# Moving the second half of an input projection behind the state product of a hybrid mixer

## The chip, the cores and the metric

The kernel runs on one core of one Trainium2 chip. The metric is the device time of one execution in microseconds (us); lower is better. The core has a matmul engine (TensorE, PE in the rows; its weight loads are PEld), VectorE (DVE), ScalarE (ACT), GpSimd (POOL), and SyncE (SP), which issues the weight transfers. PE writes its results into eight PSUM banks, numbered 0 to 7.

## The reference, cut to what matters

The program is a two-layer network followed by a second network whose first layer holds a hybrid mixer. Only that mixer is touched. For 256 tokens (two tiles of 128) it computes:

```python
def hybrid_mixer(h, w_in, conv_w, ...):
    z, xbc, dt_raw, q, k, v, f_raw = jnp.split(h @ w_in, offs, axis=-1)
    xbc = jax.nn.silu(causal_conv(xbc, conv_w, conv_b))
    xs, bm, cm = jnp.split(xbc, ...)
    y = ssd_chunked(xh, dt, a, bm, cm)        # state-space branch
    y = (y + d_skip * xh) * silu(z)           # then normed: y_ssm
    o = forgetting_attention(q, k, v, log_f)  # 8 heads of 128, causal
    return jnp.concatenate([y_ssm, o], axis=-1) @ w_out

def forgetting_attention(q, k, v, log_f):     # per block of 128 queries
    logits = q @ k * d ** -0.5 + cum[query] - cum[key]
    return softmax(where(causal, logits, -inf)) @ v
```

## The kernel before

**Products.** Every product is in f32 out of two rounded halves: a weight block is cut into an upper part (ScalarE, the `cut` of `scalar_program`) and a rest (VectorE, the `cut` of `vector_program`), and `three` issues three matmuls: upper by upper, upper by rest, rest by upper. Weights come in halves of 128x1024. One half of a 512-column block is 12 matmuls (two row groups `f`, two token tiles, three products). `W.span["hyb.z7"]` are the four halves of the last input block, and `W.span["hyb.out0"]` are the first halves of the output product. Four slots hold cut weights, so a half is cut at most three ahead of its use (`cut_ahead`).

**The mixer.** The input product has the blocks z0 to z7. Blocks z2 and z3 are the queries, z4 and z5 the keys, z6 and z7 the values; z7 holds the values of heads 4 to 7. Small pieces of work stand between the halves of z4 to z7, listed in the tables called `work` on each of the three engines, by number 4*(block-4)+half. After z7 PE runs `within(0)` (first tile of the state-space branch), the state product (event `hyb.S0`, banks 0 and 1), `within(1)`, the product with the state (`hyb.yo`), and then the attention, by hand, unit by unit. A unit is four heads of one query tile: units 0 and 1 are heads 0 to 3, units 2 and 3 heads 4 to 7; odd units have 256 keys, even ones 128. `front(i)` is the scores on PE, scale, bias and maximum on VectorE (events `fox{i}.sc`, `fox{i}.max`), the exponentials on ScalarE (`fox{i}.p`); `middle(i)` transposes the weights on PE and copies them out on ScalarE; `back(i)` is the product with the values. `queries(hg)` and `keys(hg)` transpose queries and keys (copies by `turned` on ScalarE); `y_parts` transposes the normed state-space rows, and `y_hi` and `y_lo` cut them; `out_halves` is the output product; `added` on VectorE builds the additive bias of the scores.

**What sets the order.** Each engine runs its own list in order. `free(banks)` makes PE wait until the last result in a bank was read; `held` notes who reads it. For scores that is VectorE's `fox{i}.sc`. The state product waits, besides its inputs, for banks 0 and 1, where the scores of unit 0 lie.

Of the kernel before, what the change touches and what calls it, by code (L numbers as in the profile page):

```python
# [17 lines left out]
P = 128  # L18
# [206 lines left out]
def build(nc, io, learned):  # L225
# [203 lines left out]
        return [dict(name=f"{l}.xat{t}", scale=P ** -0.5, add=None, dv=P, nk=TT, t=t, place=IN_ORDER,  # L429
                     value=lambda h, kt: z[:, kt, XV + h * P:XV + (h + 1) * P], dst=heads(ostage[:, t, :], 4)) for t in range(TT)]  # L430

    QT, KTs = [ostage[:, :, :].rearrange("p t (a n) -> p (t a) n", a=2), tT[:, 8:12, :]], [acc[:, 0:4, :], nT[:, 4:8, :]]
    xt = [z[:, t, H_X:H_X + D] for t in range(TT)]
    R = [[tT[:, 12 + 4 * t:16 + 4 * t, :] for t in range(TT)], [xt[t].rearrange("p (h k) -> p h k", h=4) for t in range(TT)]]
    heads_out = [[ostage[:, t, :] for t in range(TT)], [z[:, t, H_Q:H_Q + 512] for t in range(TT)]]

    def fox_units():
        return [dict(name=f"fox{2 * hg + t}", scale=P ** -0.5, add=R[hg][t][:, :, 0:(t + 1) * P], dv=P, nk=t + 1, t=t, hg=hg, place=IN_ORDER,
# [58 lines left out]
    def tensor_program():  # L497
# [171 lines left out]

            return lambda c, t: buf[:, t, at + c * P:at + (c + 1) * P]  # L670

        def attention(units, scores, ready, values=(), first=None, beside={}, by_act=False, between=None, amid={}, rear_banks=(6, 7), behind={}, within={}, by_hand=False):

            n_ = len(units)

            def front(i):
                b = 2 * (i % 2)
                free(b, b + 1)
                for p in ready(i):
                    PE.wait_ge(*p)  # L680
                o = ps[:, b:b + 2, :].rearrange("p a (h k) -> p (a h) k", h=2)
                u_ = units[i]
                scores(u_, o).then_inc(*psum_full.up(f"{u_['name']}.s"))
                held(act_out.at(f"{u_['name']}.p") if u_["add"] is None else dve_out.at(f"{u_['name']}.sc"), b, b + 1)

            def middle(i):
                s, n = i % 2, units[i]["name"]
                PE.wait_ge(*act_out.at(f"{n}.p"))
                free(4, 5)
                nk = units[i]["nk"]  # L690
                for h in range(4):
                    for kt in range(nk):
                        m = PE.transpose(ps[:, 4 + h // 2, (h % 2 * nk + kt) * P:(h % 2 * nk + kt + 1) * P], S[:, s, h, kt * P:(kt + 1) * P], ident)  # L693
                m.then_inc(*psum_full.up(f"{n}.t"))
                held(act_out.at(f"{n}.PT") if by_act else dve_out.at(f"{n}.PT"), 4)
                held(act_out.at(f"{n}.PT"), 5)

            def back(i):
                s, b, u_ = i % 2, rear_banks[i % len(rear_banks)], units[i]
                n, dv, nk = u_["name"], u_["dv"], u_["nk"]  # L700
                if not by_act:
                    PE.wait_ge(*dve_out.at(f"{n}.PT"))
                PE.wait_ge(*act_out.at(f"{n}.PT"))
                free(b)
                for p in values:
                    PE.wait_ge(*p)
                for h in range(4):
                    for kt in range(nk):
                        m = PE.matmul(ps[:, b, h * dv:(h + 1) * dv], PTs[:, s, nk * u_["place"][h] + kt, :], u_["value"](h, kt), start=(kt == 0), stop=(kt == nk - 1))  # L709
                    if h == 1 and i in within:  # L710
                        within[i]()
                m.then_inc(*psum_full.up(f"{n}.o"))
                held(dve_out.at(f"{n}.out"), b)

            if by_hand:
                return front, middle, back

            front(0)
            if between:
                between()  # L720
            front(1)
            if first:
                first()

            def rear(i):
                back(i)
                if i in beside:
                    beside[i]()
            for i in range(n_):
                middle(i)  # L730
                if i in amid:
                    amid[i]()
                if i + 2 < n_:
                    front(i + 2)
                if i + 2 in behind:
                    behind[i + 2]()
                if i:
                    rear(i - 1)
            rear(n_ - 1)
# [369 lines left out]
        def hybrid(then):  # L1109
# [54 lines left out]
            def to_rows(t):  # L1164
                PE.wait_ge(*act_out.at("hyb.silu"))
                for q, (first, n_) in enumerate(row_sets):
                    b = row_banks[q]
                    free(b)
                    for i in range(n_):
                        m = PE.transpose(ps[:, b, i * P:(i + 1) * P], tT[:, first + i, TOK[t]], ident)  # L1170
                    m.then_inc(*psum_full.up(f"hyb.rows{t}{q}"))
                    held(act_out.at(f"hyb.rows{t}{q}"), b)
# [12 lines left out]
            def keys(hg):  # L1185
                turn(f"hyb.K{hg}", cols_of(z, H_K + 512 * hg), 4, [act_out.at(f"hyb.z{4 + hg}")], lambda c: act_out.at(f"hyb.K{hg}.{c}"))

            work = {0: sums, 2: lambda: to_rows(0), 5: lambda: to_rows(1), 7: products, 12: lambda: queries(0), 13: lambda: keys(0)}
            def scores(u_, o):
                for h in range(4):  # L1190
                    keys_ = slice(0, u_["nk"] * P)
                    m = PE.matmul(o[:, h, keys_], QT[u_["hg"]][:, h, TOK[u_["t"]]], KTs[u_["hg"]][:, h, keys_], start=True, stop=True)
                return m
            front, middle, back = attention(fox_units(), scores, lambda i: [act_out.at(f"hyb.K{i // 2}.2"), act_out.at(f"hyb.Q{i // 2}.2")], by_act=True,
                                            rear_banks=(0, 7, 6, 7), by_hand=True)
            work[15] = lambda: front(0)
            for b in range(4, 8):
                banks = (2 * (b % 2), 2 * (b % 2) + 1)
                gemm(f"hyb.z{b}", lhs, banks, beside=lambda n_: work.get(4 * (b - 4) + n_, lambda: None)())
                held(act_out.at(f"hyb.z{b}"), *banks)  # L1200

            def within(t):
                PE.wait_ge(*dve_out.at(f"hyb.W{t}"))
# [15 lines left out]
            held(act_out.at("hyb.S0"), 0, 1)  # L1219
            within(1)  # L1220
            PE.wait_ge(*act_out.at("hyb.S0"))
            free(2, 3)
            for g in range(2):
                m = PE.matmul(ps[:, 2 + g, :], CT[:, g, P:2 * P], S0[:, g * 512:(g + 1) * 512], start=True, stop=True)
            m.then_inc(*psum_full.up("hyb.yo"))
            held(dve_out.at("hyb.yo"), 2, 3)


            def out_halves(first, last):
# [13 lines left out]
            def y_parts(*groups_):  # L1243
                for c in groups_:
                    part_group("hyb.yT", cols_of(z), 8, c, [act_out.at("hyb.ynorm"), dve_out.at("hyb.ynorm")], (6, 7, 1, 3))
            queries(1)
            keys(1)
            front(1)
            middle(0)
            front(2)  # L1250
            front(3)
            middle(1)
            y_parts(0, 2)
            back(0)
            y_parts(4)
            middle(2)
# [121 lines left out]
    def vector_program():  # L1378
# [152 lines left out]
            V.tensor_tensor(block_of(x, hf), block_of(x, hf), o, ALU.add).then_inc(*dve_out.up(event))  # L1531


        def attention(units, out, first=None, beside={}, by_act=False, between=None, second=None, amid={}, rear_banks=(6, 7), by_hand=False):

            def front(i):
                s, b, u_ = i % 2, 2 * (i % 2), units[i]
                keys = slice(0, u_["nk"] * P)
                n, o = u_["name"], ps[:, b:b + 2, :].rearrange("p a (h k) -> p (a h) k", h=2)[:, :, keys]
                Su, nm = S[:, s, :, keys], rs[:, s, 0, :]  # L1540
# [450 lines left out]
        def hybrid():  # L1991
# [64 lines left out]
            def added(hg, tokens=range(TT)):  # L2056
                own()
                V.wait_ge(*keys_loaded.at(hg))
                for t in tokens:
# [6 lines left out]

            work = {0: sums, 4: lambda: state_inputs(0), 5: lambda: decays(0), 7: lambda: decays(1), 8: lambda: state_inputs(1), 9: lambda: skipped(0), 10: to_end,
                    11: lambda: weigh(0), 12: lambda: skipped(1), 13: lambda: weigh(1), 14: lambda: added(0)}
            for b in range(4, 8):
                cuts(f"hyb.z{b}", lambda n: work.get(4 * (b - 4) + n, lambda: None)())  # L2070

            def within(t):
                V.wait_ge(*psum_full.at(f"hyb.y{t}"))
                own()
                for g in range(2):
                    V.tensor_tensor(xt[t][:, g * 512:(g + 1) * 512], xt[t][:, g * 512:(g + 1) * 512], ps[:, y_banks[t][g], :], ALU.add).then_inc(*dve_out.up(f"hyb.y{t}{g}"))
            front, middle, back = attention(fox_units(), plain_out, by_act=True, rear_banks=(0, 7, 6, 7), by_hand=True)
            own()
            front(0)
            within(0)  # L2080
# [1 line left out]
            own()  # L2082
            V.tensor_tensor(z[:, 0, 0:D], z[:, 0, 0:D], xt[0], ALU.mult).then_inc(*dve_out.up("hyb.zy0"))
            V.wait_ge(*psum_full.at("hyb.yo"))
            V.tensor_tensor(heads(yo), ps[:, 2:4, :].rearrange("p a (h d) -> p (a h) d", h=8), bc(eacs, 64), ALU.mult).then_inc(*dve_out.up("hyb.yo"))

            def second_tokens():
                own()
# [153 lines left out]
    def scalar_program():  # L2242
# [460 lines left out]
        def hybrid():  # L2703
# [63 lines left out]

            def last_decays():
                decays(1, 11, 16)
                turned("Q", 0, QT)  # L2770

            def products():
# [3 lines left out]
            def turned(kind, hg, dst):  # L2776
                for c in (0, 2):
                    pair_to(f"hyb.{kind}{hg}", c, dst[hg][:, c:c + 2, :], 6 + c // 2)

            work = {0: sums, 2: lambda: to_rows(0), 3: spread_rows, 5: lambda: to_rows(1), 6: lambda: decays(0, 0, 4), 7: first_half, 8: lambda: decays(0, 8, 12), 9: lambda: decays(0, 12, 16),  # L2780
                    10: lambda: decays(1, 0, 6), 11: lambda: decays(1, 6, 11), 12: last_decays, 13: lambda: turned("K", 0, KTs)}
            for b in range(4, 8):
                cuts(f"hyb.z{b}", lambda n: work.get(4 * (b - 4) + n, lambda: None)())
                A.wait_ge(*product(f"hyb.z{b}"))
                scaled(f"hyb.z{b}", block_of(z, 3 + b), ps[:, 2 * (b % 2):2 * (b % 2) + 2, :])
            A.wait_ge(*psum_full.at("hyb.S0"))
            A.copy(S0, ps[:, 0:2, :].rearrange("p a b -> p (a b)")).then_inc(*act_out.up("hyb.S0"))
            def y_squares(t):
# [27 lines left out]
            front(1)  # L2816
            y_parts()
            middle(1)
            front(2)
            y_hi(0, 2)  # L2820
            y_hi(4)
# [383 lines left out]
```

## Time and profile before

| | us |
|---|---|
| runs, median of 3 | 2071.18 |
| runs, lowest and highest | 2071.17 and 2074.01 |
| profiled execution, its own time | 2073.56 |
| span of the profiled execution | 2072.1 |
| granted clock of the profiled execution, mean | 0.997 |

The span runs from the first instruction to the last one; the 1.5 us between it and the execution's own time lie around it. All times in rows count from the start of the span. The part that is changed lies between 1334 and 1392 us.

### The profile page before, as it was taken

How to read it: one execution, taken by the hardware profiler on the slowest of the kernel's cores; microseconds unless marked ns; L12 is line 12 of the kernel's file. 1: busy time of each engine (PE TensorE's matmuls, PEld its weight loads, DVE VectorE, ACT ScalarE, POOL GpSimd, SP SyncE). 2: the span in 40 equal slices, each digit the busy share in tenths (PEclk: the TensorE clock that was granted, in tenths of full speed). 3: DMA queues.
4: the chain of work that ended last, by engine and by line, in shares of the span. 5: the costliest groups of instructions: out<-in, count | busy, mean ns of one | idle time of the engine just before them, and what ended most of it. 6: DMA issues, size and time to landing. Idle time of an engine off the chain costs nothing.

```text
span 2072.1 us, 27212 instructions
## 1 busy us (share of the span) xinstructions
PE 2044.6 (99%) x10690; PEld 1723.7 (83%) x10690; DVE 1431.9 (69%) x2056; ACT 1180.3 (57%) x1906; POOL 65.8 (3%) x101
## 2 busy tenths in 40 slices
PE   9999999999999999999999999999999999999998
PEld 7877888888887788888888888878888888887887
DVE  6987756764698875676577557776765766587763
ACT  5547566553546656555465457755554655486552
POOL 0001100000000200000000000000000000010000
PEclk9999999999999999999999999999999999999999
DMA  7572344555555244455455554515555555545553
GB/s 251 198 247 100 144 164 149 191 196 183 186 202 213 92 163 158 154 198 183 183 203 193 185 212 183 214 68 195 185 184 200 186 192 186 203 151 192 186 199 123
DMA packets 54902, 372.56 MB, mean 180 GB/s; under 512 B 7471, under 2 KB 7767, under 8 KB 11128
## 3 DMA queue, kind: packets, MB, share of 16 engines
q1 hardware_dynamic: 49392, 356.54, 47.5%
q10 hardware_dynamic: 4872, 12.70, 1.9%
q0 software_dynamic: 512, 1.57, 0.3%
q8 instruction: 86, 1.41, 0.3%
q14 instruction: 40, 0.33, 0.0%
HBM read 369.46 MB, written 1.34 MB: 179 GB/s over the span
## 4 chain that ended last, share of the span: by engine, by line
PE 92%; ACT 3%; DVE 3%; DMA 1%; issue 1%; POOL 0%; SPq 0%; DVEq 0%; ACTq 0%; POOLq 0%
PE ps L567 21%; PE ps L519 17%; PE ps L523 17%; PE ps L520 17%; PE ps L573 11%; PE ps L709 1%; DMA ring<-in_w 1%; PE ps L602 1%; PE ps L642 1%; PE ps L658 1%; PE ps L693 1%; DVE ring_lo L1386 1%; ACT S L2392 1%; ACT upper_w L2254 0%; PE ps L1207 0%
## 5 line engine op out<-in xcount | busy, mean ns | idle before, releaser
L1386 DVE TENSOR_TENSOR ring_lo<-ring,upper_w 128x1024 fp32r<-128x1024 f32 x435 | 525.4, 1222 | 202.7 <-ACT upper_w L2254 201.6
L2254 ACT CAST upper_w<-ring 128x1024 fp32r<-128x1024 f32 x435 | 449.3, 1050 | 277.6 <-DMA ring<-in_w 163.3
L520 PE MATMUL ps<-ring_lo,nT_pair 128*128 128x512 f32 (+1 forms) x984 | 382.2, 388 | 0.0
L519 PE MATMUL ps<-upper_w,nT_pair 128*128 128x512 f32 (+1 forms) x848 | 337.4, 398 | 2.2 <-DVE ring_lo L1386 1.5
L523 PE MATMUL ps<-upper_w,nT_pair 128*128 128x512 f32 (+1 forms) x680 | 265.4, 390 | 0.0
L573 PEld LDWEIGHTS ps<-nT_pair,ring_lo 128*128 128x128 f32 x1920 | 246.2, 191 | 9.4
L573 PE MATMUL ps<-nT_pair,ring_lo 128*128 128x256 f32 x1920 | 249.0, 283 | 0.0
L520 PE MATMUL ps<-ring_lo,z_hi 128*128 128x512 f32 x624 | 242.9, 389 | 0.0
L567 PE MATMUL ps<-nT_pair,upper_w 128*128 128x512 f32 x960 | 230.0, 391 | 0.0
L520 PEld LDWEIGHTS ps<-ring_lo,nT_pair 128*128 128x128 f32 x984 | 185.6, 189 | 35.3
L567 PEld LDWEIGHTS ps<-nT_pair,upper_w 128*128 128x128 f32 x960 | 176.5, 188 | 34.2
L523 PE MATMUL ps<-upper_w,tT_lo 128*128 128x512 f32 (+1 forms) x528 | 204.8, 388 | 0.0
L519 PEld LDWEIGHTS ps<-upper_w,nT_pair 128*128 128x128 f32 x848 | 159.9, 189 | 38.6 <-issue 3.5
L1386 DVE TENSOR_TENSOR ring_lo<-ring,PT_w 128x1024 fp32r<-128x1024 f32 x112 | 134.9, 1220 | 55.2 <-ACT PT_w L2254 55.2
L1386 DVE TENSOR_TENSOR ring_lo<-ring,S_w 128x1024 fp32r<-128x1024 f32 x112 | 134.7, 1219 | 46.5 <-ACT S_w L2254 46.5
L2254 ACT CAST PT_w<-ring 128x1024 fp32r<-128x1024 f32 x112 | 115.5, 1050 | 70.0 <-DMA ring<-in_w 70.0
L2456 ACT COPY z<-ps 128x512 f32<-128x512 f32 x60 | 35.2, 587 | 207.6 <-PE ps L573 207.6
L523 PEld LDWEIGHTS ps<-upper_w,nT_pair 128*128 128x128 f32 x680 | 127.9, 188 | 27.3 <-DVE nT_pair L1448 0.7
L1618 DVE TENSOR_TENSOR acc<-ps,z 128x512 f32<-128x512 f32 x60 | 41.5, 692 | 156.0 <-ACT z L2456 156.0
L2254 ACT CAST S_w<-ring 128x1024 fp32r<-128x1024 f32 x112 | 115.5, 1050 | 55.8 <-DMA ring<-in_w 55.6
L519 PE MATMUL ps<-upper_w,z_hi 128*128 128x512 f32 x360 | 142.1, 395 | 0.0
L520 PEld LDWEIGHTS ps<-ring_lo,z_hi 128*128 128x128 f32 x624 | 117.3, 188 | 23.4
(389 smaller groups left out, 2876.7 us busy)
## 6 DMA issues: line engine op xcount, KB each, us to landing
ring<-in_w SPq DMA_DIRECT2D x338, 1024.0 KB, 4.8
big<-in_gains ACTq DMA_DIRECT2D x7, 512.0 KB, 4.2
z<-in_mem ACTq DMA_DIRECT2D x2, 1024.0 KB, 7.5
big<-skew POOLq DMA_DIRECT2D x8, 192.0 KB, 6.7
x<-in_x SPq DMA_DIRECT2D x2, 512.0 KB, 7.4
ring<-in_w SPq DMA_DIRECT2D x2, 512.0 KB, 7.0
PTs<-skew ACTq DMA_DIRECT2D x1, 1024.0 KB, 4.6
big<-skew ACTq DMA_DIRECT2D x1, 1024.0 KB, 8.8
```

Source lines behind the costliest of these rows:

```text
L519: PE.matmul(out, hi, w_hi, start=start, stop=False)
L520: PE.matmul(out, hi, w_lo, start=False, stop=False)
L523: return PE.matmul(out, lo, w_hi, start=False, stop=stop)
L567: PE.matmul(ps[:, base + i, :], upper(W.halves[h][2])[:, cols], nT_pair[:, :, 2 * c + k, :], start=(c == 0 and k == 0), stop=False)
L573: m = PE.matmul(ps[:, base + i, 0:T], w_lo[:, cols], nT_hi[:, 2 * c + k, :], start=False, stop=(2 * c + k == KT - 1))
L602: m = PE.transpose(ps[:, b, i * P:(i + 1) * P], src[:, t, (4 * g + i) * P:(4 * g + i + 1) * P], ident)
L642: m = PE.transpose(ps[:, b, (i * TT + t) * P:(i * TT + t + 1) * P], src(c + i, t), ident)
L658: m = PE.transpose(ps[:, b, (i * TT + t) * P:(i * TT + t + 1) * P], src(c + i, t), ident)
L1386: V.tensor_tensor(ring_lo[:, q % RING, cols], ring[:, q % RING, cols], upper(n).bitcast(F32), ALU.subtract).then_inc(*lo_cut.up(h))
L1618: V.tensor_tensor(pair(b), ps[:, base:base + 2, 0:T], ffn_half[:, 0:2, :], ALU.add).then_inc(*dve_out.up())
L2254: A.copy(upper(n), ring[:, q % RING, part * HALF:(part + 1) * HALF]).then_inc(*hi_cut.up(h))
L2456: A.copy(ffn_half[:, 0:2, :], ps[:, base:base + 2, T:2 * T]).then_inc(*act_out.up(f"{f}.hg{b}"))
```

## The change

The last two halves of z7 leave the loop over the input blocks. PE now runs: z4 to z6; `queries(0)`; the first half of z7; `keys(0)`; the second half; `front(0)`; `within(0)`, the state product, `within(1)`, `hyb.yo`; the third half of z7; `queries(1)`, `keys(1)`, `front(1)`, `middle(0)`, `front(2)`; the fourth half; `middle(1)`, `y_parts(0, 2)`, and only then `front(3)`. Since z7 sums up in banks 2 and 3 over this whole time, `hyb.yo` moves to banks 0 and 1, and the units' scores lie in the banks that start at 0, 0, 0 and 2. ScalarE reads z7 out (`scaled`) between `middle(1)` and `front(2)`. The cuts: during z7 only two are made (the fourth half of z7, the first of the output product); the second and third half of the output product are cut where so far only the fourth was, after `y_hi(6)` and `y_lo(6)`. The transposed keys of heads 4 to 7 move from `nT`, which the late halves still read, to the second tile of `xn`.

```diff
--- before.py
+++ after.py
@@ -429,10 +429,12 @@
-    QT, KTs = [ostage[:, :, :].rearrange("p t (a n) -> p (t a) n", a=2), tT[:, 8:12, :]], [acc[:, 0:4, :], nT[:, 4:8, :]]
+    QT, KTs = [ostage[:, :, :].rearrange("p t (a n) -> p (t a) n", a=2), tT[:, 8:12, :]], [acc[:, 0:4, :], xn[:, 1, :].rearrange("p (c n) -> p c n", n=T)]
     xt = [z[:, t, H_X:H_X + D] for t in range(TT)]
...
     heads_out = [[ostage[:, t, :] for t in range(TT)], [z[:, t, H_Q:H_Q + 512] for t in range(TT)]]
+
+    FOX_BANKS = (0, 0, 0, 2)
@@ -669,12 +671,12 @@
-        def attention(units, scores, ready, values=(), first=None, beside={}, by_act=False, between=None, amid={}, rear_banks=(6, 7), behind={}, within={}, by_hand=False):
+        def attention(units, scores, ready, values=(), first=None, beside={}, by_act=False, between=None, amid={}, rear_banks=(6, 7), behind={}, within={}, by_hand=False, front_banks=None):
...
             def front(i):
-                b = 2 * (i % 2)
+                b = 2 * (i % 2) if front_banks is None else front_banks[i]
                 free(b, b + 1)
@@ -1185,19 +1187,35 @@
-            work = {0: sums, 2: lambda: to_rows(0), 5: lambda: to_rows(1), 7: products, 12: lambda: queries(0), 13: lambda: keys(0)}
+            work = {0: sums, 2: lambda: to_rows(0), 5: lambda: to_rows(1), 7: products, 11: lambda: queries(0)}
             def scores(u_, o):
...
             front, middle, back = attention(fox_units(), scores, lambda i: [act_out.at(f"hyb.K{i // 2}.2"), act_out.at(f"hyb.Q{i // 2}.2")], by_act=True,
-                                            rear_banks=(0, 7, 6, 7), by_hand=True)
-            work[15] = lambda: front(0)
-            for b in range(4, 8):
+                                            rear_banks=(0, 7, 6, 7), by_hand=True, front_banks=FOX_BANKS)
+            for b in range(4, 7):
                 banks = (2 * (b % 2), 2 * (b % 2) + 1)
...
                 held(act_out.at(f"hyb.z{b}"), *banks)
+
+            def last_values(c):
+                h = W.span["hyb.z7"][c]
+                w_hi, w_lo = weights(h)
+                if c == 0:
+                    free(2, 3)
+                for k in range(2):
+                    f, cols = 2 * c + k, slice(k * BLK, (k + 1) * BLK)
+                    for t in range(TT):
+                        m = three(ps[:, 2 + t, :], lhs[0](f, TOK[t]), lhs[1](f, TOK[t]), w_hi[:, cols], w_lo[:, cols], f == 0, f == KT - 1)
+                m.then_inc(*half_used.up(h))
+                if c == 3:
+                    held(act_out.at("hyb.z7"), 2, 3)
+            last_values(0)
+            keys(0)
+            last_values(1)
+            front(0)
@@ -1219,11 +1237,11 @@
             PE.wait_ge(*act_out.at("hyb.S0"))
-            free(2, 3)
+            free(0, 1)
             for g in range(2):
-                m = PE.matmul(ps[:, 2 + g, :], CT[:, g, P:2 * P], S0[:, g * 512:(g + 1) * 512], start=True, stop=True)
+                m = PE.matmul(ps[:, g, :], CT[:, g, P:2 * P], S0[:, g * 512:(g + 1) * 512], start=True, stop=True)
             m.then_inc(*psum_full.up("hyb.yo"))
-            held(dve_out.at("hyb.yo"), 2, 3)
+            held(dve_out.at("hyb.yo"), 0, 1)
@@ -1243,14 +1261,16 @@
                     part_group("hyb.yT", cols_of(z), 8, c, [act_out.at("hyb.ynorm"), dve_out.at("hyb.ynorm")], (6, 7, 1, 3))
+            last_values(2)
             queries(1)
...
             front(2)
-            front(3)
+            last_values(3)
             middle(1)
             y_parts(0, 2)
+            front(3)
             back(0)
@@ -1531,10 +1551,10 @@
-        def attention(units, out, first=None, beside={}, by_act=False, between=None, second=None, amid={}, rear_banks=(6, 7), by_hand=False):
+        def attention(units, out, first=None, beside={}, by_act=False, between=None, second=None, amid={}, rear_banks=(6, 7), by_hand=False, front_banks=None):
...
             def front(i):
-                s, b, u_ = i % 2, 2 * (i % 2), units[i]
+                s, b, u_ = i % 2, 2 * (i % 2) if front_banks is None else front_banks[i], units[i]
                 keys = slice(0, u_["nk"] * P)
@@ -2066,15 +2086,19 @@
                     11: lambda: weigh(0), 12: lambda: skipped(1), 13: lambda: weigh(1), 14: lambda: added(0)}
-            for b in range(4, 8):
+            for b in range(4, 7):
                 cuts(f"hyb.z{b}", lambda n: work.get(4 * (b - 4) + n, lambda: None)())
+            for n, h in enumerate(W.span["hyb.z7"]):
+                if n < 2:
+                    cut_ahead(h)
+                work.get(12 + n, lambda: None)()
...
                     V.tensor_tensor(xt[t][:, g * 512:(g + 1) * 512], xt[t][:, g * 512:(g + 1) * 512], ps[:, y_banks[t][g], :], ALU.add).then_inc(*dve_out.up(f"hyb.y{t}{g}"))
-            front, middle, back = attention(fox_units(), plain_out, by_act=True, rear_banks=(0, 7, 6, 7), by_hand=True)
+            front, middle, back = attention(fox_units(), plain_out, by_act=True, rear_banks=(0, 7, 6, 7), by_hand=True, front_banks=FOX_BANKS)
             own()
@@ -2082,7 +2106,7 @@
             V.wait_ge(*psum_full.at("hyb.yo"))
-            V.tensor_tensor(heads(yo), ps[:, 2:4, :].rearrange("p a (h d) -> p (a h) d", h=8), bc(eacs, 64), ALU.mult).then_inc(*dve_out.up("hyb.yo"))
+            V.tensor_tensor(heads(yo), ps[:, 0:2, :].rearrange("p a (h d) -> p (a h) d", h=8), bc(eacs, 64), ALU.mult).then_inc(*dve_out.up("hyb.yo"))
@@ -2767,6 +2791,10 @@
                 decays(1, 11, 16)
+                turned("K", 0, KTs)
+
+            def more_decays():
+                decays(1, 6, 11)
                 turned("Q", 0, QT)
@@ -2778,11 +2806,14 @@
             work = {0: sums, 2: lambda: to_rows(0), 3: spread_rows, 5: lambda: to_rows(1), 6: lambda: decays(0, 0, 4), 7: first_half, 8: lambda: decays(0, 8, 12), 9: lambda: decays(0, 12, 16),
-                    10: lambda: decays(1, 0, 6), 11: lambda: decays(1, 6, 11), 12: last_decays, 13: lambda: turned("K", 0, KTs)}
-            for b in range(4, 8):
+                    10: lambda: decays(1, 0, 6), 11: more_decays}
+            for b in range(4, 7):
                 cuts(f"hyb.z{b}", lambda n: work.get(4 * (b - 4) + n, lambda: None)())
...
                 scaled(f"hyb.z{b}", block_of(z, 3 + b), ps[:, 2 * (b % 2):2 * (b % 2) + 2, :])
+            cut_ahead(W.span["hyb.z7"][0])
+            last_decays()
+            cut_ahead(W.span["hyb.z7"][1])
             A.wait_ge(*psum_full.at("hyb.S0"))
@@ -2816,6 +2847,8 @@
             middle(1)
+            A.wait_ge(*product("hyb.z7"))
+            scaled("hyb.z7", block_of(z, 10), ps[:, 2:4, :])
             front(2)
```

## Rows read from the trace of the kernel before

**Rows 1.** First part of the page: busy us, share, instructions.
```profile
PE 2044.6 (99%) x10690; PEld 1723.7 (83%) x10690; DVE 1431.9 (69%) x2056; ACT 1180.3 (57%) x1906; POOL 65.8 (3%) x101
```
**Rows 2.** PE's timeline: start us, us, engine, line, operation, operands, count [idle before].
```profile
1337.10 1.03 PE L642 MATMUL ps<-const,z 128*128 128x128 f32 x8
...
1340.71 1.04 PE L642 MATMUL ps<-const,z 128*128 128x128 f32 x8
...
1347.08 1.06 PE L1192 MATMUL ps<-acc,ostage 128*128 128x128 f32 x8
1347.97 3.68 PE L1207 MATMUL ps<-xn,PTs 128*128 128x64 f32 x32
1351.49 1.94 PE L1217 MATMUL ps<-big,z 128*128 128x512 f32 x4
...
1358.55 1.04 PE L642 MATMUL ps<-const,z 128*128 128x128 f32 x8
...
1360.82 1.89 PE L1192 MATMUL ps<-acc,ostage 128*128 128x256 f32 x8
```
**Rows 3.** Windows: stretch, length, busy PE, PEld, DVE, ACT, POOL, granted clock, DMA.
```profile
140.00:142.00 2.00, 2.00 (x10) 1.51 (x8) 2.00 (x4) 1.08 (x2) 0.00 (x0) 0.50 1.02 418
...
1364.00:1368.00 4.00, 2.26 (x11) 1.53 (x9) 3.93 (x9) 3.52 (x12) 1.01 (x1) 1.00 0.01 2
...
1372.00:1375.00 3.00, 1.01 (x7) 0.70 (x7) 2.06 (x5) 2.77 (x9) 0.00 (x0) 1.00 0.01 3
1375.60:1379.00 3.40, 3.40 (x17) 3.30 (x16) 2.91 (x6) 1.98 (x8) 0.00 (x0) 0.50 0.02 5
```
**Rows 4.** The chain of waits, 1363 to 1378: start us, us, engine and line.
```profile
1363.88 1.15 DVE S L1543
...
1366.31 2.08 ACT S L2392 x8
1368.38 1.23 ACT z L2806 x2
1369.61 0.98 ACT PTs L2399
1370.58 1.54 ACT S L2392 x8
...
1372.94 1.67 DVE tT_lo L1427 x4
1374.75 2.97 PE ps L709 x16
```
**Rows 5.** ScalarE's timeline before the state product.
```profile
1335.84 1.25 ACT L2370 ACTIVATE z<-ps,st 128x512 f32<-128x512 f32 x2
1336.98 1.04 ACT L2254 CAST upper_w<-ring 128x1024 fp32r<-128x1024 f32 x1
1337.93 1.57 ACT L2762 ACTIVATE big<-big,cbuf 128x128 f32<-128x128 f32 x5
1339.40 1.05 ACT L2380 COPY ostage<-ps 128x512 f32<-128x512 f32 x2
1340.34 1.06 ACT L2254 CAST upper_w<-ring 128x1024 fp32r<-128x1024 f32 x1
```
**Rows 6.** VectorE's timeline before the state product.
```profile
1338.06 1.23 DVE L1386 TENSOR_TENSOR ring_lo<-ring,upper_w 128x1024 fp32r<-128x1024 f32 x1
...
1341.43 1.23 DVE L1386 TENSOR_TENSOR ring_lo<-ring,upper_w 128x1024 fp32r<-128x1024 f32 x1 [1.01 <-ACT upper_w L2254]
1342.57 2.35 DVE L2053 TENSOR_TENSOR big<-big,acc 128x1024 f32<-128x1024 f32 x2
...
1345.98 2.84 DVE L2064 SCALAR_TENSOR_TENSOR tT<-tT,cbuf,const 128x128 f32<-128x128 f32 x8
1348.73 1.22 DVE L1386 TENSOR_TENSOR ring_lo<-ring,upper_w 128x1024 fp32r<-128x1024 f32 x1
1349.87 0.69 DVE L1543 SCALAR_TENSOR_TENSOR S<-ps,tT 128x512 f32<-128x512 f32 x1
```

## The prediction

> **What bounds the kernel now.** I read the page first: PE is busy for 99% of the span [rows 1], so a change pays only where PE stands still or runs at its lower clock. The timeline of PE, the windows and the chain of waits then show where that is. Up to the product with the state PE has no pause: it goes from the last half of z7 through the scores of unit 0, `within(0)` and the state product in unbroken steps [rows 2]. Behind it PE thins out: from 1364 to 1368 us it is busy for 2.26 of 4.00 us, from 1372 to 1375 for 1.01 of 3.00 us, and there the chain of waits runs over ScalarE and VectorE [rows 3, 4]. After the second of these the granted clock is 0.50 from 1375.6 to 1379.0, the 1.2 GHz level [rows 3]. VectorE and ScalarE, by contrast, are packed before the state product: their pieces follow each other without a gap, but for one wait of 1.01 us of VectorE for a cut of ScalarE [rows 5, 6]. So the change takes PE work out of a stretch in which the other two engines are the slower ones, and puts it into one in which PE has holes.
>
> **Prices of PE's steps** [rows 2]. From 1337.10 to 1340.71 stand eight turns and one half of z7: 3.61 us. From 1340.71 to 1347.08 stand eight turns and two halves: 6.37 us. So a half is 2.76 us and eight turns 0.85 us. `front(0)` is 0.89 us (1347.08 to 1347.97), `within` 3.52 us (to 1351.49), and 7.06 us lie from the state product to the turns of the second queries (1358.55). No half is added or taken away; two, 5.52 us, are moved. What counts is which pauses come and go.
>
> **First place: the state product.** PE after the change, from the end of z6 at 1337.10 - 2.76 = 1334.34: turns of queries 0 to 1335.19, first half of z7 to 1337.95, turns of keys 0 to 1338.80, second half to 1341.56, `front(0)` to 1342.45, `within(0)` to 1345.97. There the state product would start, 5.52 us earlier than at 1351.49. But it needs banks 0 and 1, which hold the scores of unit 0 until VectorE has read them. In the old order that was done at 1349.87 + 0.69 = 1350.56, just in time [rows 6].
>
> How far VectorE moves forward: ScalarE first. The copy of queries 0 (0.94 us, 1339.40 to 1340.34) now stands ahead of the reading of z6, and the copy of keys 0 (as large, 0.95 us) ahead of the first cut of the output product. ScalarE starts its queries at 1335.84, reads z6 from 1336.78, cuts the last half of z7 from 1337.92, takes the decays to 1340.34, keys 0 to 1341.29, and only then starts the cut of `hyb.out0` that started at 1340.34 before [rows 5]. VectorE can begin its own part 1.09 us after such a start (1340.34 to 1341.43), so at 1342.38 instead of 1341.43 [rows 6]. From there its list is a cut (1.14), `weigh(1)` (2.27: from 1342.57 to 1345.98 are 3.41, less a cut), `added(0)` (2.75), and the score (0.69). The second and third cut of the output product are gone from between them, 2 x 1.14 us. So the score starts at 1342.38 + 1.14 + 2.27 + 2.75 = 1348.54 and ends at 1349.23. With 0.1 us for the signal PE starts the state product at 1349.33. It stands still for 1349.33 - 1345.97 = 3.36 us, where it had no pause. Gained there are 2.16 us, not 5.52.
>
> The Trainium skill (PSUM — Partial Sum Buffer, section Engine vs sequencer instructions) says that VectorE's and ScalarE's queues are strictly first in, first out. By this rule the pause is the 3.36 us above; if `added(0)` and the score could pass `weigh(1)`, which only `within(1)` needs, it would be 2.27 us shorter. The order of starts in the trace agrees.
>
> **Second place: from the product with the state to the output product.** Everything from the state product on comes 2.16 us earlier, until the third half of z7 (2.76 us) is put in: the second queries' turns start at 1358.55 - 2.16 + 2.76 = 1359.15, and `front(1)`, at 1360.82 before, at 1361.42 [rows 2]. VectorE's sums after `hyb.yo` run during that half and end before, near 1361.7 (1363.88 - 2.16 [rows 4]), so the score of unit 1 now waits for PE: 1361.42 + 1.89 = 1363.3 to 1364.5 (1.15), maximum to 1365.8 (1.23), exponentials to 1367.9 (2.08) [rows 2, 4]. PE does `middle(0)` (four turns, 0.43) and waits for the score until 1364.6, 0.9 us, as units 1 and 2 now share banks. `front(2)` (0.9) and the fourth half (2.76) end at 1368.3. So the exponentials of unit 1, for which PE stood still before, are hidden: `middle(1)` runs at once, to 1369.15, and `y_parts`, whose rows ScalarE has normed by 1369.15 (1.23 [rows 4]), to 1370.0.
>
> Then the added wait: `front(3)` needs banks 2 and 3, and ScalarE reads z7 from them only after its copy for `middle(1)` (0.98 [rows 4], to 1370.2); the reading takes 1.25 us [rows 5], to 1371.45. Before, it lay at the end of z7 under PE's work. PE stands still for 1.4 us. Queued behind it on ScalarE are the exponentials of unit 2 (1.54, to 1373.0) and `y_hi`; `y_lo` follows 0.82 us after their end and takes 1.67 us [rows 4], to 1375.5. PE meanwhile does `front(3)` (1.89, to 1373.4), `back(0)`, four turns and `middle(2)` (0.9 + 0.43 + 0.43, to 1375.2) and starts `back(1)` at 1375.6, after 0.4 us. At 0.11 us an instruction (32 in 3.52 us [rows 2]) its 16 take 1.76 us, and four turns bring PE to 1377.8. VectorE still owes the score (1.15), the maximum (1.23) and the output of unit 0 (0.69) that frees bank 0: 1375.5 + 3.07 = 1378.6. PE waits 0.8 us and starts the output product at 1378.65. Before, `back(1)` ran from 1374.75 for 2.97 us at the low clock [rows 4], and its four turns at twice 0.43 ended at 1378.6. The sum at this place is therefore 0.0 us.
>
> **Third place: the output product.** Its second half is now cut behind `y_hi(6)`: exponentials of unit 3 from 1377.9 to 1380.0, two cuts of `y_hi` (0.7), the cut on ScalarE (1.06 [rows 5]), then VectorE's (1.23 [rows 6]), about 1383.1. PE needs it after one half, `middle(3)` and `back(2)`: 1378.65 + 2.76 + 0.85 + 0.88 = 1383.1. I take nothing, with 0 to 1 us as bounds. The moved keys, the moved banks of `hyb.yo` and the read of the key rows cost nothing: the copies are the same, and the state product's banks are read by ScalarE under `within(1)`; without that cover it would be its copy, some 1 us.
>
> **The clock.** A pause of 3.36 us behind the 64-column products of `within(0)` is longer than any that these rows show. After 1372 to 1375, with 1.99 us idle, the clock fell; after 1364 to 1368, with 1.74 us idle, it stayed at 1.00, and a fall to 0.50 is also seen at 140 to 142 us [rows 3]. So I take it that it falls, now on the state product and `within(1)`, where PE is the only engine on the path. Price: `back(1)` took 2.97 us for 1.76, and its turns doubled, 1.6 us in all [rows 4]; 3.4 us at half speed are 1.7 us [rows 3]. Bounds are 0 (it stays) and 1.9; since a part may fall into the pause, 1.5 us.
>
> The Trainium skill (TensorE: Matmul & The Clock Gate, section HAM oscillation) says that a wait between bursts of matmuls throttles the clock, and the next burst starts cold. By this rule the sum is +1.5 us, without it 0.0. That a fall follows a thin stretch the trace shows; a pause of this length it does not.
>
> **Sum.** 0.0 + 1.5 = +1.5 us. The profiled execution took 2073.56 us, 2.4 us over the median of the runs, 2071.18; I put the 1.5 us on the median: 2072.7 us. This kernel's measurement tells about 0.2%, 4.1 us, from no change, so I forecast no change.
>
> **Rivals.**
> 1. The pause is there, the clock stays up: 0.0, 2071.2 us. For it speaks that the clock stayed up through 1364 to 1368; against it the pause's length. 24%.
> 2. The pause does not form, because VectorE reaches the score of unit 0 before PE is through `within(0)`. That would give back 3.36 us: 2067.8 us. VectorE would have to finish its list 3.3 us earlier, while ScalarE hands it the cut later; against that stand the packed lists [rows 5, 6]. 13%, of which 4% with the wait for z7 gone too, past 4.1 us.
> 3. Slower: the clock falls at the pause and stays down through the state product, `within(1)` and `hyb.yo`, as these are small products. Their 7.06 us would double: 2071.2 + 7.1 = 2078.3 us. It decides if over 4.1 us of them run low. Against it: `within` at full clock had 1.00 before, and the low stretch in [rows 3] ended after 3.4 us. 7%.
> 4. The late cuts hold PE up as well: +1 us on the forecast, 2073.7 us. 6%.
>
> The forecast has 50%, its own range 2071.0 to 2074.0. The range of all: rival 2 and the errors of the steps reach down to 2069.4, the late cuts, two falls of the clock and the spread of the runs (2071.17 to 2074.01) up to 2075.0. Faster by over 0.2%: 4%; within: 89%; slower: 7%.
>
> **What would show it.** Right: PE idle for about 3.4 us ahead of the state product, ended by VectorE's score; a wait near 1.4 us before `front(3)`, ended by ScalarE's reading of z7; `middle(1)` without its wait for ScalarE; the clock at 0.50 behind the state product's pause and no longer at the output product. Wrong: a state product that starts at `within(0)`'s end, or a wait of PE for `ring_lo` at the second half of the output product that is over 1 us.

## The result, and the profile after the change

| | kernel before | changed kernel |
|---|---|---|
| runs, median of 20 | 2071.62 us | 2074.64 us |
| runs, lowest and highest | 2070.62 and 2074.35 us | 2073.53 and 2079.02 us |
| ratio, 95% interval | | 1.0017 (1.0011 to 1.0023) |

The change made the kernel slower, by 3.0 us between the medians. The forecast of 2072.7 us had the sign, half the size, and called it no change; the interval over 20 runs of each kernel lies wholly above 1.

First the timeline of PE after the change, over the moved work. Line numbers are higher by the lines that were added: 2 for turns, scores and `back`, 18 for the state-space products, 20 on VectorE, 24 on ScalarE. (1341.04 answers to `within(0)`, 1348.16 to the state product, 1359.69 and 1361.96 to the second queries' turns and `front(1)` in [rows 2]; 1368.96 is `middle(1)`, 1379.26 and 1383.78 are the first two halves of the output product.)

```profile
1332.79 1.03 PE L644 MATMUL ps<-const,z 128*128 128x128 f32 x8
...
1336.41 1.04 PE L644 MATMUL ps<-const,z 128*128 128x128 f32 x8
...
1340.08 1.13 PE L1194 MATMUL ps<-acc,ostage 128*128 128x128 f32 x8
1341.04 3.68 PE L1225 MATMUL ps<-xn,PTs 128*128 128x64 f32 x32
1348.16 3.24 PE L1235 MATMUL ps<-big,z 128*128 128x512 f32 x4 [3.44 <-DVE S L1563]
1351.20 4.12 PE L1225 MATMUL ps<-xn,big 128*128 128x64 f32 x32
1355.15 1.94 PE L1242 MATMUL ps<-nT,tT 128*128 128x512 f32 x4
...
1359.69 1.03 PE L644 MATMUL ps<-const,z 128*128 128x128 f32 x8
...
1361.96 1.89 PE L1194 MATMUL ps<-acc,ostage 128*128 128x256 f32 x8
...
1365.22 1.13 PE L1194 MATMUL ps<-xn,tT 128*128 128x128 f32 x8 [0.93 <-DVE S L1563]
...
1368.96 1.04 PE L695 MATMUL ps<-const,S 128*128 128x128 f32 x8
...
1372.32 1.96 PE L1194 MATMUL ps<-xn,tT 128*128 128x256 f32 x8 [1.44 <-ACT z L2394]
...
1376.37 2.02 PE L711 MATMUL ps<-z,PTs 128*128 128x128 f32 x16 [0.33 <-DVE tT_lo L1447]
...
1379.26 0.50 PE L521 MATMUL ps<-upper_w,nT_pair 128*128 128x512 f32 x1 [0.43 <-DVE ostage L1616]
...
1383.78 0.48 PE L521 MATMUL ps<-upper_w,nT_pair 128*128 128x512 f32 x1
...
1391.29 1.03 PE L660 MATMUL ps<-const,ostage 128*128 128x128 f32 x8
```

PE stands still for 3.44 us ahead of the state product, ended by VectorE's score (`S`, line 1563). The state product then takes 3.24 us in place of 1.94 [rows 2]. The wait of 1.44 us before `front(3)` is ended by ScalarE's reading of z7. The windows around the pause (length, busy us of PE, PEld, DVE, ACT, POOL, granted clock) show the cause of the slow state product: behind the empty stretch the clock is at 0.50, the 1.2 GHz level, and then at 1.00 again. The last window is that ahead of the output product, where the kernel before had 0.50 [rows 3].

```profile
1344.60:1348.10 3.50, 0.13 (x2) 0.00 (x0) 3.40 (x10) 0.00 (x0) 0.00 (x0) 1.00 0.00 0
1348.70:1352.10 3.40, 3.40 (x9) 1.85 (x8) 2.51 (x3) 0.66 (x1) 0.00 (x0) 0.50 0.02 5
1352.10:1356.00 3.90, 3.90 (x31) 3.49 (x31) 0.00 (x0) 1.90 (x9) 0.00 (x0) 1.00 0.00 0
...
1375.00:1380.00 5.00, 4.24 (x33) 3.71 (x32) 4.96 (x9) 2.86 (x9) 0.00 (x0) 1.00 0.02 5
```

VectorE's timeline (answering to [rows 6]) shows what PE waits for. The cut at 1340.80 still waits 1.01 us for ScalarE; from there VectorE has no gap of over 0.05 us until the score.

```profile
1340.80 1.23 DVE L1406 TENSOR_TENSOR ring_lo<-ring,upper_w 128x1024 fp32r<-128x1024 f32 x1 [1.01 <-ACT upper_w L2278]
1341.94 2.35 DVE L2073 TENSOR_TENSOR big<-big,acc 128x1024 f32<-128x1024 f32 x2
1344.33 2.85 DVE L2084 SCALAR_TENSOR_TENSOR tT<-tT,cbuf,const 128x128 f32<-128x128 f32 x8
1347.21 0.69 DVE L1563 SCALAR_TENSOR_TENSOR S<-ps,tT 128x512 f32<-128x512 f32 x1
```

Executions differ by falls of the clock in other places too (at 140 to 142 us in the first profile of the kernel before [rows 3], near 1866 to 1870 us in its second, taken below), so the kernels are best compared over the stretch that the change touches: from the end of z6 to the first turn of the attention's outputs. The changed kernel reaches the one at 1332.79 (the queries' turns begin) and the other at 1391.29: 58.50 us. In the profile of the kernel before it is 1337.10 less a half of 2.76 [rows 2], to 1390.49: 56.15 us (the half's first matmul starts 0.03 us later in the trace, which changes nothing below). The stretch carries the difference: in every profile of this document the execution's own time less its stretch is 2015.4 to 2016.3 us, but for that first profile (2073.56 - 56.15 = 2017.4).

```profile
1390.49 1.04 PE L658 MATMUL ps<-const,ostage 128*128 128x128 f32 x8
```

### The profile page after: what moved, and what is told of

The parts are those of the page before. It is cut to its first block, busy times and chain, and to the rows that moved or that the text cites. A ratio compares the mean times of both kernels' runs of the same rounds, so it can differ in the third digit from the quotient of the medians.

```text
span 2072.8 us, 27212 instructions
## 1 busy us (share of the span) xinstructions
PE 2043.9 (99%) x10690; PEld 1721.5 (83%) x10690; DVE 1432.5 (69%) x2056; ACT 1180.4 (57%) x1906; POOL 65.8 (3%) x101
## 4 chain that ended last, share of the span: by engine, by line
PE 91%; ACT 4%; DVE 3%; DMA 1%; issue 1%; POOL 0%; SPq 0%; DVEq 0%; ACTq 0%; POOLq 0%
PE ps L569 21%; PE ps L521 17%; PE ps L525 17%; PE ps L522 17%; PE ps L575 11%; DMA ring<-in_w 1%; PE ps L711 1%; PE ps L604 1%; PE ps L644 1%; PE ps L695 1%; PE ps L660 1%; ACT upper_w L2278 1%; DVE ring_lo L1406 1%; DVE S L1563 0%; ACT S L2416 0%
```

## The experiments

The theory: the pause ahead of the state product, which VectorE's list makes, and the fall of the clock behind it are the loss. The rival: the later waits make it (scores that share banks, the reading of z7, the late cuts). Each kernel, 11 runs if nothing else is said, was timed beside the kernel before on the same chip; the third column is the median of those runs of the kernel before. The ratio is an estimate of its own, with its interval, and not the quotient of the two medians. The stretch is that of the section above, each from one profile.

| kernel | median, us | before, us | ratio (95%) | stretch, us | low clock in the stretch |
|---|---|---|---|---|---|
| kernel before, first profile, 20 runs | 2071.62 | | | 56.15 | output product |
| changed kernel, 20 runs | 2074.64 | 2071.62 | 1.0017 (1.0011 to 1.0023) | 58.50 | state product |
| pause filled | 2072.22 | 2071.22 | 1.0001 (0.9993 to 1.0010) | 56.68 | none |
| third half in the pause | 2071.56 | 2071.22 | 1.0002 (0.9993 to 1.0010) | 56.65 | fourth half |
| z7 read by VectorE | 2074.10 | 2071.22 | 1.0014 (1.0006 to 1.0023) | 57.80 | state product, 6.8 us |
| third half, z7 by VectorE | 2070.38 | 2071.22 | 0.9994 (0.9985 to 1.0003) | 53.93 | none |
| the same again | 2070.34 | 2071.36 | 0.9997 (0.9988 to 1.0006) | 53.94 | none |
| score before `weigh(1)` | 2071.85 | 2071.51 | 1.0001 (0.9993 to 1.0010) | 56.10 | state product |
| score first, z7 by VectorE | 2073.83 | 2071.51 | 1.0009 (1.0000 to 1.0018) | 54.55 | none |
| banks alone | 2071.75 | 2071.51 | 1.0003 (0.9995 to 1.0012) | 56.14 | output product |
| kernel before again, second profile | 2071.28 | 2071.51 | 0.9999 (0.9990 to 1.0008) | 55.28 | none |
| kernel before, third profile, one run | 2071.54 | 2071.36 | | 56.14 | output product |
| all three edits | 2068.95 | 2071.36 | 0.9991 (0.9982 to 1.0000) | 53.04 | none |
| the same again | 2069.36 | 2071.52 | 0.9991 (0.9982 to 1.0000) | 53.03 | none |

### The pause filled with work that nothing reads

```diff
             PE.wait_ge(*act_out.at("hyb.rows02"))
+            free(4, 5)
+            for i in range(12):
+                PE.matmul(ps[:, 4 + i % 2, :], nT_hi[:, 0, TOK[0]], nT_hi[:, 2:4, :].rearrange("p c n -> p (c n)"), start=True, stop=True)
             free(0, 1)
```

> The changed kernel with twelve matmuls more, whose result nothing reads, put into PE's pause ahead of the state product (12 x 0.23 = 2.8 us into 3.4 us). The state product starts when it did. Theory A (the clock's fall after the pause is the larger part of the loss): the clock stays at 1.00 there, the state product, within(1) and hyb.yo take 7.1 us instead of 8.7, and the time falls by 1.6 us against the changed kernel, to about +1.4 us over the kernel before. Theory B (the loss lies in the later waits: banks shared by the scores, the reading of z7, the late cuts): the time stays at +3 us over the kernel before.

PE's timeline, and the window over the state product:

```profile
1343.68 3.01 PE L1235 MATMUL ps<-nT_pair 128*128 128x512 f32 x12
1347.20 1.96 PE L1238 MATMUL ps<-big,z 128*128 128x512 f32 x4 [0.51 <-DVE S L1566]
```
```profile
1347.20:1350.50 3.30, 3.30 (x18) 2.34 (x19) 3.09 (x4) 1.31 (x4) 0.00 (x0) 1.00 0.02 5
```

The state product still waits for VectorE, but at 1.00 it is back at 1.96 us. The stretch is 58.50 - 56.68 = 1.82 us shorter, with no useful work moved; the median lies 1.0 us over the kernel before in place of 3.0, and the intervals of the two kernels do not overlap. Of the 1.82 us, 0.11 come from a state product that starts earlier (15.26 us after the end of z6 in place of 15.37); the other 1.71 are the price of the fall. So the fall of the clock is shown as the larger part of the loss. What is left of it, 56.68 - 56.15 = 0.53 us (1.40 against the profile of the kernel before that has no fall in the stretch, 55.28), is the pause and the later waits together, less what the moved halves hide.

### The third half in the pause

```diff
             within(0)
+            last_values(2)
             PE.wait_ge(*dve_out.at("hyb.Xd"))
...
-            last_values(2)
             queries(1)
```

> The changed kernel with the third half of z7 between within(0) and the state product; only the fourth half stays late. Theory A (the pause and its clock): pause down to about 0.6 us, no fall of the clock, VectorE's sums after hyb.yo start some 1.6 us earlier, the second queries' turns 4.4 us earlier; VectorE's sums then end the wait for the score of unit 1, as before the change, so about 3 us are won: 0 us against the kernel before. Theory B (later waits): the waits behind hyb.yo stay or grow and it remains 2 us or more over the kernel before.

```profile
1347.58 1.96 PE L1236 MATMUL ps<-big,z 128*128 128x512 f32 x4 [0.63 <-DVE S L1563]
...
1361.23 1.44 PE L1194 MATMUL ps<-xn,tT 128*128 128x128 f32 x8 [1.72 <-DVE S L1563]
```
```profile
1361.90:1365.30 3.40, 3.40 (x12) 2.81 (x11) 3.33 (x11) 2.96 (x11) 1.01 (x1) 0.50 0.00 0
```

The loss is gone: 0.3 us in the median, an interval around 1. Real work fills the pause as well as idle work did. The expected absence of a fall did not come: in its profile the clock fell later (0.50 from 1361.9 to 1365.3), behind a wait of 1.72 us that now stands before `front(2)`. The same order has 53.9 us, below, without that fall and with z7 read elsewhere.

### z7 read by VectorE, alone and with the third half

```diff
-                    held(act_out.at("hyb.z7"), 2, 3)
+                    held(dve_out.at("hyb.z7"), 2, 3)
...
-            A.wait_ge(*product("hyb.z7"))
-            scaled("hyb.z7", block_of(z, 10), ps[:, 2:4, :])
...
             front(2)
+            V.wait_ge(*product("hyb.z7"))
+            for t in range(TT):
+                V.tensor_scalar(block_of(z, 10)[:, t, :], ps[:, 2 + t, :], st[:, 8 + t:9 + t], None, ALU.mult).then_inc(*dve_out.up("hyb.z7" if t else None))
             added(1, (1,))
```

> The changed kernel with z7 read out by VectorE (2 x 0.69 us, ahead of its bias for the units with heads 4 to 7) instead of ScalarE (1.25 us, ahead of the exponentials of unit 2). PE's wait of 1.44 us before front(3) has the reading as its last releaser. If ScalarE's chain behind the reading (exponentials, y_hi, y_lo) sets the output product's start, 1.1 us are won: +1.9 us over the kernel before. If PE's wait itself were all of it, PE gets front(3) about 1 us earlier and the same is won; if VectorE's own list binds, nothing is won and it stays at +3 us.

> Both of the foregoing edits: third half of z7 in the pause, z7 read out by VectorE. If the two losses are apart from each other they add up: about -4 us against the changed kernel, -1 us against the kernel before. If VectorE's list becomes the bound (it takes 1.4 us on just where it has gained 1.6 us), the sum is that of the third half alone: 0 us against the kernel before.

> The third half in the pause and z7 read out by VectorE once more, as the first interval (0.9985 to 1.0003) left open whether it is faster than the kernel before. Its stretch was 53.9 us against 55.3: -1.0 us, ratio 0.9995. Rival: the runs of the kernel before without a fall are as fast, ratio 1.0000.

PE's timeline with z7 read by VectorE alone, and the window of its low clock:

```profile
1348.29 3.75 PE L1235 MATMUL ps<-big,z 128*128 128x512 f32 x4 [3.43 <-DVE S L1563]
...
1355.76 1.94 PE L1242 MATMUL ps<-nT,tT 128*128 128x512 f32 x4
...
1372.05 1.97 PE L1194 MATMUL ps<-xn,tT 128*128 128x256 f32 x8 [0.57 <-DVE z L2138]
...
1390.72 1.03 PE L660 MATMUL ps<-const,ostage 128*128 128x128 f32 x8
```
```profile
1345.85:1352.68 6.83, 4.39 (x9) 2.36 (x9) 5.34 (x9) 0.60 (x1) 0.00 (x0) 0.50 0.01 2
```

`y_lo` of VectorE, which waits for `y_hi` of ScalarE, in the changed kernel and then in this one:

```profile
1374.57 1.66 DVE L1447 SCALAR_TENSOR_TENSOR tT_lo<-ps,sm,nT_pair 128x256 fp32r<-128x256 f32 x4 [2.83 <-ACT nT_pair L2319]
```
```profile
1374.01 1.66 DVE L1447 SCALAR_TENSOR_TENSOR tT_lo<-ps,sm,nT_pair 128x256 fp32r<-128x256 f32 x4 [0.35 <-ACT nT_pair L2322]
```

From `hyb.yo` to the outputs' turns are 1390.72 - 1355.76 = 34.96 us against 1391.29 - 1355.15 = 36.14 in the changed kernel: the 1.1 us expected are there, and in this part the rival is right. ScalarE's chain behind the reading was the bound: VectorE stood still for 2.83 us for it, and now for 0.35. The median missed: it lies 2.9 us over the kernel before, where 1.9 were expected. In this profile the clock went down inside the pause already and stayed down for 6.8 us, which takes 0.5 us back; 3 of its 11 runs took 2078 us and more, and where their clock was low is not shown. With the third half in the pause as well, no stretch is low and both gains show: 53.9 us, 0.8 and 1.0 us under the kernel before. Both intervals reach over 1, so this version is not told from the kernel before.

### The score of unit 0 before `weigh(1)`

```diff
-                    11: lambda: weigh(0), 12: lambda: skipped(1), 13: lambda: weigh(1), 14: lambda: added(0)}
+                    11: lambda: weigh(0), 12: lambda: skipped(1), 13: lambda: added(0)}
...
             front(0)
+            weigh(1)
             within(0)
```

> The changed kernel with VectorE's list in another order: bias and score of unit 0 ahead of weigh(1), which only within(1) needs. Theory A (VectorE's order holds the state product up): the score is done 2.3 us earlier, the pause ahead of the state product falls from 3.4 to 1.2 us, within(1) waits some 0.7 us for weigh(1), the clock stays up; 3.2 us are won against the changed kernel, so 0 us against the kernel before. Theory B (the pause has another cause, or is paid back behind): the state product starts when it did, or the output product does; +2 to +3 us against the kernel before.

> The foregoing edit, and z7 read out by VectorE. By theory A the third half still covers VectorE's sums behind hyb.yo, and the reading is off ScalarE's chain: 1 us less than the foregoing, -1 us against the kernel before. By theory B +1 to +2 us.

PE's timeline at the state product and the window behind it; then, with z7 read by VectorE, the state product and `within(1)`:

```profile
1345.68 3.43 PE L1235 MATMUL ps<-big,z 128*128 128x512 f32 x4 [1.04 <-DVE S L1563]
```
```profile
1346.00:1349.40 3.40, 3.40 (x7) 1.38 (x6) 3.16 (x5) 0.25 (x1) 0.00 (x0) 0.50 0.00 0
```
```profile
1344.99 1.96 PE L1235 MATMUL ps<-big,z 128*128 128x512 f32 x4 [1.04 <-DVE S L1563]
...
1348.01 3.79 PE L1225 MATMUL ps<-xn,big 128*128 128x64 f32 x32 [1.06 <-DVE big L2073]
```

VectorE's order does hold the state product: it started 1345.68 - 1332.70 = 12.98 us after the end of z6, in place of 15.37. The stretch falls by as much, 2.40 us, though the clock still falls; with the 1.7 us of the fall and the 1.2 us of the reading that is more than the whole loss. What is over is what the late halves gain, as the last version below shows. The time against the kernel before came out as expected for the first of the two, +0.3 us. But "the clock stays up" did not hold: it fell behind a pause of 1.04 us. The second missed, with +2.3 us for the -1 expected: its profiled run, without a fall in the stretch, has the shorter stretch expected (54.55 us), but of its 11 runs only 4 took 2070.3 to 2071.5 us at a mean clock of 0.998 or 0.999; the other 7 took 2072.9 to 2077.1 at 0.996 or 0.997. It has two pauses of 1 us, on either side of the state product; that the clock falls behind them in those 7 runs would fit, but where it was low in them is not shown.

### The banks alone

```diff
+    FOX_BANKS = (0, 0, 0, 2)
...
-            free(2, 3)
+            free(0, 1)
...
-                m = PE.matmul(ps[:, 2 + g, :], CT[:, g, P:2 * P], S0[:, g * 512:(g + 1) * 512], start=True, stop=True)
+                m = PE.matmul(ps[:, g, :], CT[:, g, P:2 * P], S0[:, g * 512:(g + 1) * 512], start=True, stop=True)
```

> The kernel before with only the banks of the change: hyb.yo in banks 0 and 1, scores in the banks that start at 0, 0, 0 and 2. All halves of z7 stay in place. If sharing banks costs, front(2) waits for the score of unit 1 where front(3) did: PE's wait of 0.8 us moves ahead by one scores step and grows to 1.9 us, but the wait for the exponentials of unit 1 behind it shrinks as much. By theory A 0 us against the kernel before; if bank sharing is a cause of the loss, +1 us or more.

```profile
1363.20 2.86 PE L1193 MATMUL ps<-nT,tT 128*128 128x128 f32 x16 [1.72 <-DVE S L1544]
1366.52 1.10 PE L694 MATMUL ps<-const,S 128*128 128x128 f32 x8 [0.46 <-ACT S L2393]
```

As expected: the wait for the score grows to 1.72 us, the one for the exponentials shrinks to 0.46 (1.35 in all three profiles of the kernel before), and the stretch is 56.14 us, that of the kernel before with the same fall of the clock. The rival's first part falls.

### The kernel before, for its clock

> The kernel before against itself, for the granted clock of each of its runs. If its fall of the clock at the output product (1375.6 us, price 1.6 us) comes in every run, all its runs have a mean clock as low as the profiled one of 0.997; if it comes in some only, part of its runs have 0.998 or more and are 1.5 us faster, and the changed kernel, whose fall comes at the long pause, is compared with a kernel that mostly has none there.

> One more profile of the kernel before, for where its clock falls. Of two profiles one had the fall at the output product (stretch of 56.15 us) and one had none (55.28 us). If the fall belongs to the kernel, it is there again; if it comes and goes, it is an even chance.

`back(1)` in the second profile, with the start of the output product, then in the third:

```profile
1372.21 2.02 PE L709 MATMUL ps<-z,PTs 128*128 128x128 f32 x16 [1.92 <-DVE tT_lo L1427]
...
1375.10 0.53 PE L519 MATMUL ps<-upper_w,nT_pair 128*128 128x512 f32 x1 [0.43 <-DVE ostage L1596]
```
```profile
1372.78 2.79 PE L709 MATMUL ps<-z,PTs 128*128 128x128 f32 x16 [1.92 <-DVE tT_lo L1427]
```

Behind the same wait of 1.92 us the clock fell in two of three profiles of this kernel. It cost 56.15 - 55.28 = 0.87 us, not the 1.6 that its instructions lost, since without it PE runs into VectorE's output of unit 0 and waits 0.43 us. The 11 runs of the second row have a mean clock of 0.998 or 0.999, none the 0.997 of the first profile.

### All three edits

Third half in the pause, z7 read by VectorE, score before `weigh(1)`, as in the diffs above.

> The three edits together: third half of z7 in the pause, z7 read out by VectorE, bias and score of unit 0 ahead of weigh(1). PE's last wait ahead of the state product (0.6 us) goes, and weigh(1) is done before PE needs it. From the end of z6 to the turns of the attention's outputs 53.3 us, against 53.9 without the third edit and 55.3 in the kernel before without a fall of the clock; no stretch at the low clock: -1.5 to -2 us against the kernel before. Rival: VectorE's sums behind hyb.yo start 0.6 us earlier, but run into weigh(1), put behind the score: 53.9 us, -1 us.

> The three edits together once more, as the first interval (0.9982 to 1.0000) just reached no change. Its stretch from the end of z6 to the turns of the attention's outputs was 53.0 us against 55.3 to 56.1 in the profiles of the kernel before: -2.2 to -3.1 us, ratio 0.9985 to 0.9990. Rival: the first median, -2.4 us, came from runs without a fall of the clock by chance; then the ratio is 0.9995 to 1.0000.

```profile
1331.76 1.03 PE L644 MATMUL ps<-const,z 128*128 128x128 f32 x8
...
1346.33 1.88 PE L1236 MATMUL ps<-big,z 128*128 128x512 f32 x4
1348.05 3.68 PE L1225 MATMUL ps<-xn,big 128*128 128x64 f32 x32
...
1384.80 1.03 PE L660 MATMUL ps<-const,ostage 128*128 128x128 f32 x8
```

PE has no pause from z6 to the state product and `within(1)`. The stretch is 53.0 us in both profiles, 53.3 expected, without a fall. The medians are 2.4 and 2.2 us under the kernel before, and all 22 runs lie under the median of the kernel before beside them; the intervals end at 1.0000, so that it is faster than the kernel before is likely rather than certain. Against the changed kernel, 3.0 us above the kernel before, it is clear.

## Why the prediction was wrong

**Right: the pause.** Forecast 3.36 us, ended by VectorE's score of unit 0; measured 3.44. The row counts from the end of the last product; from where the next one could have started, as the forecast counts, it is 3.60 us (1341.04 + 3.52 = 1344.56 to 1348.16). Moving the score forward moved the state product forward by 2.4 us, so the order of VectorE's list is shown to be the cause.

**Right: the later waits.** Before `front(2)` 0.9 forecast and 0.93 measured, before `front(3)` 1.4 and 1.44 with the reading of z7 as releaser, before `back(1)` 0.4 and 0.33; for bank 0 0.8 and 0.43, which is half; none for the exponentials of unit 1, none for the late cuts.

**Right in kind: the clock.** It fell on the state product, as forecast, and no longer ahead of the output product (1.00 from 1375 to 1380).

**Wrong: three sizes in the sum.** The step that failed is the sum; the pause, its releaser and the fall came as forecast. First, "The sum at this place is therefore 0.0 us" was 0.53: the stretch without a fall is 56.68 us, against 56.15 of the kernel before with its own fall. Of this 0.27 us lie before the state product, which starts 15.26 us after z6's end with the pause filled, not 14.99: VectorE's score began after 14.42 us, not 14.20. Before the bias and the score VectorE waits for its own last result (`own()`), and with no cut between them that is the end of the piece just ahead: the bias starts at 1344.33 behind 1341.94 + 2.35 = 1344.29, the score at 1347.21 behind 1344.33 + 2.85 = 1347.18. The forecast took the shorter steps from start to start that a cut between them had allowed.

The second is the price of the clock, "since a part may fall into the pause, 1.5 us": it was 1.82, the earlier start included, for in the profile nothing fell into the pause, where the clock is 1.00. Of the two prices behind it, 3.4 us at half speed, 1.7 us, was right (1.71); the other set `back(1)`'s row of 2.97 us against 1.76 us counted from start to start, where the row without a fall is 2.02. The first two sizes make 0.53 + 1.82 = 2.35 us where the forecast had 1.5.

Third, the sum was set against a profiled execution in which the kernel before had its own fall and then put on the median of the runs. That fall is absent in one profile of three, and against that profile the changed kernel loses 58.50 - 55.28 = 3.22 us. The measured 3.0 us lie between.

**Wrong: what can be told apart.** "0.2%, 4.1 us, from no change" was too coarse: 20 runs of each put the ratio at 1.0011 to 1.0023. The likeliest case had the right mechanism and should have been called a small loss.

**Rival 3 in part.** The clock stayed down for 6.8 us in one profile. Four of the 20 runs of the changed kernel took 2077.4 to 2079.0 us at a mean clock of 0.996; the others took 2073.5 to 2075.5 at 0.997 or 0.998. A longer low stretch would fit this, but where the clock was low in those four is not shown.

## What to carry to other kernels

Work moved out of a stretch does not make that stretch shorter where another engine sets its end: lay the other engines' lists beside the new order first, and look for who frees the bank that the next product needs. A pause made on PE can cost twice, by its length and by the clock where it falls behind it, so late work is best put into the pause itself and the engine that ends it given its blocking step first. A sum made on one profiled execution holds only for the falls of the clock that this execution had; profile the kernel before more than once when a few us count.

## What the runs showed of the hardware that was not expected

The clock fell behind a pause as short as 1.04 us next to the 64-column products (0.50 from 1346.0 to 1349.4), and yet the same pause does not always bring a fall. Of two profiles with 1.04 us ahead of the state product one has it; of six with 1.72 us before `front(2)` one; of four with 1.92 us before `back(1)` (three of the kernel before, and banks alone) three; of two with 3.43 and 3.44 us both. So a fall is better put into a sum by its chance than as certain. In the stretch studied here the clock stayed low for 3.4 us each time but one, where it was 6.8 us.
